# Five gate and up groups of three FFN layers as seven block products (Strassen form), with the pre-norm gain on the rows and h kept in DRAM

## Chip, cores and metric

One Trainium2 chip; the program runs on 1 of its cores. The metric is the device time of one execution in microseconds (us), the median of several runs. TensorE is written PE here, with PEld for its weight loads; VectorE is DVE, ScalarE is ACT, GpSimd is POOL and SyncE is SP, whose queue issues nearly all DMAs.

## What is computed

Two decoder layers over 512 tokens of width 1024. Each layer is: half-step SwiGLU FFN, token mixing, cross-attention, half-step SwiGLU FFN. So there are four FFNs. The part that the change touches:

```python
def half_ffn(h, l, j):
    y = swiglu(rms_norm(h, ffn_norm_pre[l, j]), ffn_w_gate[l, j], ffn_w_up[l, j], ffn_w_down[l, j])
    return h + 0.5 * rms_norm(y, ffn_norm_post[l, j])
def swiglu(x, w_gate, w_up, w_down):
    return (silu(x @ w_gate) * (x @ w_up)) @ w_down
# x: 512 x 1024;  w_gate, w_up: 1024 x 2816;  w_down: 2816 x 1024;  float32
```

## The kernel before

**Precision.** Every large product is made in three matmuls (`three`, lines 2109 to 2113): each operand is split into a rounded high part and a low part that holds the rest, and hi*lo, lo*hi and hi*hi are added in PSUM. So every weight piece has to be split on the chip before PE can use it: ACT copies the piece `raw` to `whi`, which rounds it (`split`, lines 780 to 796), and DVE makes `wlo` = raw - whi (`split`, lines 1306 to 1326). The input x is held as `xhi` and `xlo`, 8 tiles of 128 features by 512 tokens.

**Pieces.** All weights are cut into numbered pieces of 128 partitions x 1024 floats. SP loads a piece into one of four `raw` slots as two DMAs of 256 KB (`load`, line 534, issued at line 541), once the low part of the piece four before it is made. ACT, DVE and PE go through the pieces in the same order. ACT and DVE work three pieces ahead of PE (LOOKAHEAD); `whi` and `wlo` have four slots, so ACT can begin piece n when PE has finished piece n-4 (`pieces_used`). PE waits for the low part of each piece (`weights`, line 2406). Each engine runs its instructions strictly in the order written, so an instruction that waits holds back all that stand behind it on its engine.

**An FFN.** The 2816 hidden columns are 11 groups of 256. A group of gate and up is 4 pieces; a piece holds 2 of the 8 feature tiles, for 256 gate and 256 up columns. PE makes 2 x 4 column blocks x 3 = 24 matmuls of 128x512 per piece (`body` line 2478, `feature_major` line 2410), 96 per group, into four PSUM banks; two sets of banks alternate. Behind the group ACT takes silu of the gate half (line 1070), DVE multiplies it with the up half (line 1752), and the result `mid` is split in its turn. The groups come in three runs (FF_GROUPS): groups 0 to 2, then a pass `quads` that multiplies them with w_down in a Strassen form; groups 3 to 5 and a second `quads`; groups 6 to 10, whose `mid` is split plainly into `plain_hi` (ACT, line 1076) and `plain_lo` (DVE, line 1769), and then `down`, which multiplies these by w_down, adds what the quads left and ends the sub-layer.

**The pre-norm.** Three of the four FFNs (all but the first) are `scaled_rows`: when the sub-layer before them ends (`close_sublayer`, lines 852 and 1453), DVE updates h tile by tile (`update`, line 1501), ACT squares it, POOL takes the power (line 697), and ACT writes h * rstd into `y_rows` (`scale_rows`, line 877, its instruction is line 879). PE transposes the four tiles (`scaled_units`, line 2201, the matmuls are line 2193), tiles 2 and 3 of them within the first group of the FFN (`first_group`, line 2316), which runs on halves of the tokens, so with 128x256 matmuls. The gain vector of the pre-norm is not in the rows: it is multiplied into the weights, as a per-partition scale when ACT and DVE split a piece (lines 795 and 1324, two instructions of 512 elements each; a piece without a gain takes one of 1024, lines 791 and 1319).

Of the kernel before, what the change touches and what calls it, by code (L numbers as in the profile page):

```python
# [61 lines left out]
S1, S2, S3, S4, A12, A22, A11 = range(7)  # L62
NEG = -1e30
# [64 lines left out]
def build(nc, A, out):  # L128
# [18 lines left out]
    NB = 4 * SEQ  # L147
    h = place("h", [P, TT, D])
    y_at = top[0]
    y = place("y", [P, KT, SEQ])  # L150
    y_rows = place("y_rows", [P, TT, D], f32, y_at)
    x_at = top[0]
# [10 lines left out]
    h_scratch = place("h_scratch", [P, D], f32, ring_at + D * FLOAT)  # L163
    rsb = place("rsb", [P, SEQ])
    ident = place("ident", [P, P])
# [30 lines left out]
    post_gain = place("post_gain", [P, D], f32, at(7 * NB))  # L196
    level_f = place("level_f", [P, P], f32, at(7 * NB + 1024))
# [10 lines left out]
    w11 = place("w11", [P, 3, GC], f32, at(2 * MID + 2048))  # L208
    w21 = place("w21", [P, 3, GC], f32, at(7 * NB + 1024))
# [52 lines left out]
    paired = lambda t: t.rearrange("p (a b) n -> p a (b n)", b=2)  # L262
    blocks_of = lambda b0, b1: PS[:, b0:b1, :].rearrange("p a (b j) -> p (a b) j", j=P)


    def sem(name):
# [8 lines left out]
    hi_made, lo_made, pieces_used = map(sem, ("hi_made", "lo_made", "pieces_used"))  # L275

# [13 lines left out]
        "var_ready", "rstd_ready", "rstd_in_split", "mean_ready", "spread_ready", "spread_used"))  # L290

# [31 lines left out]
    STAGES = stages()  # L323

# [21 lines left out]
    def group_pieces(kind, g, n, arg=None):  # L346

        return 1 if kind == "odd_in" and ODD_COLS[g][0] == "c_f" else \
            n + 2 if arg == "late_kv" and g == 0 else n

    total_pieces = sum(group_pieces(kind, g, n, arg) for kind, _, arg, ng, n in STAGES for g in range(ng))

# [24 lines left out]
    def scaled_rows(kind, l, arg):  # L377

        return kind == "gate_up" and (l, arg[0]) != (0, 0)

# [15 lines left out]
    for kind, _, arg, ng, n in STAGES:  # L396
        if kind != "quads":
            for _ in range(sum(group_pieces(kind, g, n, arg) for g in range(ng))):
                raw_of.append(len(raw_split))
                raw_split.append(len(raw_of) - 1)  # L400
# [3 lines left out]
        raw_split += [place_of("B22", min(q + 1, QUADS - 1)) for q in range(0, QUADS, 2)]  # L404
        raw_of += [None] * n

# [49 lines left out]
    for kind, l, arg, ng, n in STAGES:  # L456
        for g in range(ng):
            for i in range(group_pieces(kind, g, n, arg)):
                gated = kind == "gate_up" or from_h(kind, arg)
# [55 lines left out]
    def _(sp):  # L515
# [18 lines left out]
        def load(n, halves):  # L534
# [3 lines left out]
            if n >= RAW_SLOTS:  # L538
                sp.wait_ge(lo_made, raw_split[n - RAW_SLOTS] + 1 + RAW_SLOTS)
# [3 lines left out]
        def load_corners(k, l, j, corners=range(3)):  # L543
# [5 lines left out]
            else:  # L549
                sp.wait_ge(lo_made, passes[k - 1][0] + len(quad_pieces()) + RAW_SLOTS)  # L550
# [52 lines left out]

        piece = ended = loads = 0
        for kind, l, arg, ng, np_ in STAGES:
            first_piece = piece
            if kind == "gate_up":
                j, n = arg
                g0 = FF_GROUPS[n][0]
                for g in range(ng):  # L610
                    for kp in range(4):
# [6 lines left out]
                        load(loads, gate_and_up(l, j, kp, (g0 + g) * 256))  # L618
                        loads += 1
                        if piece and piece + 4 * ng in pass_of and g == (2 if n == 0 else 1) and kp < 3:  # L620
                            load_corners(pass_of[piece + 4 * ng], l, j, (kp,))
                    if g == ng - 1 and not piece:
                        load_corners(0, l, j)
                piece += 4 * ng
# [33 lines left out]
            if ends_sublayer(kind, arg):  # L658
                sp.wait_ge(pieces_used, first_piece + 1 + SPLIT_SLOTS)
                if ended:  # L660
                    sp.wait_ge(post_gain_used, ended)
                sp.dma_start(post_gain[:], post_gain_rows(kind, l, arg).broadcast_to([P, D])).then_inc(post_gain_loaded, 16)
                ended += 1
        assert piece == total_pieces
# [10 lines left out]
    def _(pool):  # L675
# [58 lines left out]
        for n_stage, (kind, l, arg, ng, np_) in enumerate(STAGES):  # L734
            base_piece = E.piece
            E.piece += sum(group_pieces(kind, g_, np_, arg) for g_ in range(ng))
# [39 lines left out]
    def _(act):  # L776
# [3 lines left out]
        def split(n):  # L780
# [6 lines left out]
            act.wait_ge(raw_full[from_slot], 32 * (raw_of[n] // RAW_SLOTS + 1))  # L787
            act.wait_ge(pieces_used, n + 1)
            gains = piece_gain[n]
# [62 lines left out]
        def close_sublayer(kind, n, n_stage):  # L852
# [197 lines left out]

        mids = sums = 0
        for n_stage, (kind, l, arg, ng, np_) in enumerate(STAGES):
# [5 lines left out]
            if kind == "gate_up":  # L1058
                for g in range(ng):
                    for kp in range(4):  # L1060
                        if early and g == 0 and kp == 0:
                            E.piece += 1
                        else:
                            split_next()
                    mids += 1
                    if scaled_rows(kind, l, arg):
# [7 lines left out]
                    if arg[1] == len(FF_GROUPS) - 1:  # L1074
                        act.wait_ge(product_ready, mids)
                        a(plain_hi[:, 2 * g:2 * g + 2, :], paired(mid[:, 4:8, :]), ACT.Copy).then_inc(mid_hi_ready, 2)
# [1734 lines left out]
```

## Time and profile before

| what | value |
|---|---|
| median of 3 runs | 2311.55 us (2310.42 to 2313.16) |
| the profiled execution, from its first to its last instruction (its span) | 2311.2 us |
| PE busy | 2289.0 us, 99% |
| PEld busy | 1940.0 us, 84% |
| DVE busy | 1336.2 us, 58% |
| ACT busy | 977.3 us, 42% |
| POOL busy | 73.6 us, 3% |
| DMA: bytes, share of 16 engines' time on SP's queue | 217.70 MB, 29.0% |

No time other than its span is listed for the profiled execution. Busy time of an engine is the time in which at least one of its instructions runs. The "mean ns" of a matmul counts from its start to its modelled end and overlaps the next one, so the rate of PE is read from the starts in the timeline, not from that mean.

### The profile page before, as it was taken

The numbers are of one execution on the slowest core, as the hardware profiler recorded it, in microseconds if no ns is written. First come the engines' busy times: TensorE is split into PE (matmuls) and PEld (weight loads), VectorE is DVE, ScalarE is ACT, GpSimd is POOL, SyncE is SP. The second block draws the span as 40 slices with busy tenths as digits, with TensorE's granted clock in tenths as the row PEclk, the third lists the DMA queues.
The fourth block names the chain that finished last, engine by engine and source line by source line (L and its number), as shares of the span: only waits on it lengthen the run. The fifth ranks groups of instructions, "written<-read, shape, count | busy, mean of one in ns | idle before, by whom it ended". The sixth has DMA issues, their size and how long they took to land. (4 is left out here: it accounts for less than half of the span.)

```text
span 2311.2 us, 30089 instructions
## 1 busy us (share of the span) xinstructions
PE 2289.0 (99%) x11883; PEld 1940.0 (84%) x11883; DVE 1336.2 (58%) x1862; ACT 977.3 (42%) x1612; POOL 73.6 (3%) x115
## 2 busy tenths in 40 slices
PE   8999999999999999999999999999999999999998
PEld 7888888888888888888888888888878888888887
DVE  5857536596645646573355564346897574557334
ACT  5433324444444444443343433235266554444332
POOL 0000003000000000000010000000000000000000
PEclk9999999999999999999999999999999999999999
DMA  4332332311223223413323313333322222341321
GB/s 168 108 130 79 95 110 74 109 64 55 74 74 105 70 78 105 146 59 105 98 85 119 124 59 102 106 95 92 101 74 83 92 65 92 110 135 48 117 93 73
DMA packets 171650, 217.70 MB, mean 94 GB/s; under 512 B 13080, under 2 KB 123000, under 8 KB 171512
## 3 DMA queue, kind: packets, MB, share of 16 engines
q1 hardware_dynamic: 171400, 215.75, 29.0%
q8 instruction: 96, 1.57, 0.3%
q14 instruction: 42, 0.34, 0.0%
q10 hardware_dynamic: 112, 0.03, 0.0%
HBM read 213.63 MB, written 2.10 MB: 93 GB/s over the span
## 5 line engine op out<-in xcount | busy, mean ns | idle before, releaser
L2111 PE MATMUL ps<-xlo,whi 128*128 128x512 f32 (+1 forms) x2056 | 755.5, 367 | 2.1 <-DVE wlo L1324 2.1
L2112 PE MATMUL ps<-xhi,wlo 128*128 128x512 f32 (+1 forms) x2056 | 753.2, 366 | 0.0
L2113 PE MATMUL ps<-xhi,whi 128*128 128x512 f32 (+1 forms) x2056 | 753.0, 366 | 0.0
L1324 DVE SCALAR_TENSOR_TENSOR wlo<-raw,vec,whi 128x512 fp32r<-128x512 f32 (+1 forms) x488 | 340.8, 742 | 388.9 <-ACT whi L795 387.8
L795 ACT ACTIVATE whi<-raw,vec 128x512 fp32r<-128x512 f32 (+1 forms) x488 | 320.8, 709 | 445.4 <-PE ps L2113 390.5
L2111 PEld LDWEIGHTS ps<-xlo,whi 128*128 128x128 f32 x2056 | 388.6, 189 | 65.6 <-issue 2.7
L2113 PEld LDWEIGHTS ps<-xhi,whi 128*128 128x128 f32 x2056 | 388.4, 189 | 62.9
L2112 PEld LDWEIGHTS ps<-xhi,wlo 128*128 128x128 f32 x2056 | 388.6, 189 | 62.0
L1319 DVE TENSOR_TENSOR wlo<-raw,whi 128x1024 fp32r<-128x1024 f32 x104 | 126.7, 1223 | 183.1 <-ACT whi L791 182.3
L791 ACT ACTIVATE whi<-raw 128x1024 fp32r<-128x1024 f32 x104 | 109.5, 1057 | 199.7 <-PE ps L2113 199.3
L2111 PE MATMUL ps<-wlo,xhi 128*128 128x512 f32 x352 | 138.6, 394 | 1.0 <-issue 1.0
L2113 PE MATMUL ps<-whi,xhi 128*128 128x512 f32 x352 | 137.2, 390 | 0.0
L2112 PE MATMUL ps<-whi,xlo 128*128 128x512 f32 x352 | 137.1, 389 | 0.0
L2229 PE MATMUL ps<-wlo,mid_hi 128*128 128x512 f32 x336 | 131.6, 392 | 0.4 <-DVE wlo L1313 0.4
L2234 PE MATMUL ps<-whi,mid_hi 128*128 128x512 f32 x336 | 130.8, 389 | 0.0
L2233 PE MATMUL ps<-whi,mid_lo 128*128 128x512 f32 x336 | 130.8, 389 | 0.0
L2111 PE MATMUL ps<-wlo,plain_hi 128*128 128x512 f32 x320 | 125.0, 391 | 0.0
L2113 PE MATMUL ps<-whi,plain_hi 128*128 128x512 f32 x320 | 124.6, 389 | 0.0
L2112 PE MATMUL ps<-whi,plain_lo 128*128 128x512 f32 x320 | 124.5, 389 | 0.0
L814 ACT ACTIVATE whi<-w 128x512 fp32r<-128x512 f32 x144 | 83.3, 622 | 91.9 <-PE ps L2113 33.9
L1313 DVE TENSOR_TENSOR wlo<-w,whi 128x512 fp32r<-128x512 f32 x144 | 92.8, 685 | 35.3 <-ACT whi L814 34.4
L1752 DVE TENSOR_TENSOR mid<-mid,ps 128x1024 f32<-128x1024 f32 x33 | 40.3, 1221 | 111.9 <-ACT mid L1070 111.9
(291 smaller groups left out, 2909.5 us busy)
## 6 DMA issues: line engine op xcount, KB each, us to landing
raw<-ffn_w_gate_dram SPq DMA_DIRECT2D x176, 256.0 KB, 2.8
raw<-ffn_w_up_dram SPq DMA_DIRECT2D x176, 256.0 KB, 3.1
raw<-ffn_w_down_dram SPq DMA_DIRECT2D x96, 256.0 KB, 3.1
w<-ffn_w_down_dram SPq DMA_DIRECT2D x72, 256.0 KB, 5.3
raw<-xattn_w_kv_dram SPq DMA_DIRECT2D x64, 256.0 KB, 2.9
raw<-even_w_in_dram SPq DMA_DIRECT2D x56, 256.0 KB, 2.9
raw<-odd_w_in_dram SPq DMA_DIRECT2D x42, 256.0 KB, 2.9
raw<-xattn_w_q_dram SPq DMA_DIRECT2D x32, 256.0 KB, 3.0
```

Of the source, the lines that this page charges most:

```text
L791: a(flat(whi[:, slot]), flat(raw[:, from_slot]), ACT.Copy).then_inc(hi_made, 1)
L795: last = a(hi[:, k, :], full[:, k, :], ACT.Copy, scale=vec[:, c:c + 1])
L814: last = a(whi[:, slot, i, :], unit_source(k, name, q), ACT.Copy)
L1313: last = v.tensor_tensor(wlo[:, slot, i, :], unit_source(k, name, q), whi[:, slot, i, :].bitcast(f32), SUB)
L1319: v.tensor_tensor(flat(wlo[:, slot]), flat(raw[:, from_slot]), flat(whi[:, slot]).bitcast(f32), SUB).then_inc(lo_made, 1)
L1324: last = v.scalar_tensor_tensor(out=lo[:, k, :], in0=full[:, k, :], scalar=vec[:, c:c + 1], in1=hi[:, k, :].bitcast(f32), op0=MUL, op1=SUB)
L2111: mm(out_ap, lh, rl, start=start, stop=False, skip_group_check=skip_group_check)
L2112: mm(out_ap, ll, rh, start=False, stop=False, skip_group_check=skip_group_check)
L2113: return mm(out_ap, lh, rh, start=False, stop=stop, skip_group_check=skip_group_check)
L2229: opening = mm(out, hi, wlo[:, slot, i, :], start=fresh, stop=False, skip_group_check=True)
L2233: mm(out, lo, whi[:, slot, i, :], start=False, stop=False, skip_group_check=True)
L2234: last = mm(out, hi, whi[:, slot, i, :], start=False, stop=ends, skip_group_check=True)
```

## The change

For the five groups 6 to 10 of the three `scaled_rows` FFNs (15 groups) the product of x with the group's gate and up columns is made in seven block products in place of eight. The four corners are: x halves by features and by tokens, and weight corners B11 (upper 512 features, gate), B12 (upper, up), B22 (lower, up), B21 (lower, gate). A group is then seven units B11, T1, T2, B21, T3, B22, T4, each a piece of 128 x 1024 floats; T1 = B12 - B11, T2 = B22 - T1, T3 = T2 - B11 and T4 = B21 - T2 are made in place in the `raw` slots by DVE (`sum_corners`). A unit is 4 x 2 x 3 = 24 matmuls of 128x256 on a half of the tokens, from x itself or from one of four sums of corners of x (`s_hi`, `s_lo`). PE's new `weave`:

```diff
+            unit("B11", x, True, True)
+            unit("T1", z, True, True)
+            pe.wait_ge(product_kept, 3 * w + 1)
+            unit("T2", x, False, True)
+            unit("B21", y, True, True)
+            pe.wait_ge(product_kept, 3 * w + 3)
+            unit("T3", x, False, True)
+            unit("B22", z, False, True)
+            pe.wait_ge(c22_ready, w + 1)
+            unit("T4", x, False, True)
```

ACT (`keep` copies a product from PSUM to SBUF; `split_next` splits the unit three ahead):

```diff
+            split_next()
+            if held_mid is not None:
...
+                    plain_high(g, held)
...
+            keep(0, c11[:], x_out)
+            split_next()
...
+            keep(1, c22[:], z_out)
+            split_next()
+            act.wait_ge(mid_lo_ready, 2 * (mids - 1))
+            keep(2, c12, x_out)
+            split_next()
+            split_next()
+            act.wait_ge(c11_ready, w + 1)
+            a(c11[:], c11[:], ACT.Silu).then_inc(c11_silu, 1)
+            split_next()
+            split_next()
+            act.wait_ge(pieces_used, base + len(WOVEN_UNITS) + SPLIT_SLOTS)
+            a(c21, x_out, ACT.Silu).then_inc(gate_silu, 1)
```

DVE (its `split_next` also makes the sum for the unit four ahead):

```diff
+            split_next()
+            if held_mid is not None:
+                if plain:
+                    plain_low(g, held)
...
+            split_next()
...
+            split_next()
+            split_next()
+            dve.wait_ge(product_kept, 3 * w + 1)
+            unit_done("B21")
+            v.tensor_tensor(c11[:], y_out, c11[:], ADD).then_inc(c11_ready, 1)
+            split_next()
+            dve.wait_ge(product_kept, 3 * w + 2)
+            unit_done("T3")
+            v.tensor_tensor(c22[:], x_out, c22[:], ADD).then_inc(c22_ready, 1)
+            split_next()
+            dve.wait_ge(product_kept, 3 * w + 3)
+            unit_done("B22")
+            E.run(v.tensor_tensor(c12, z_out, c12, ADD))
...
+            v.tensor_tensor(u12, c11[:], c12, MUL)
+            split_next()
+            dve.wait_ge(gate_silu, mids).then_inc(bank_free[bank // 4], 1)
+            dve.wait_ge(c22_ready, w + 1)
+            v.tensor_tensor(c21, c21, c22[:], MUL).then_inc(product_ready, 1)
```

The low parts of B11, B21 and B22 are not made by DVE: ACT writes -raw into `wlo` ahead of its copy to `whi`, and POOL adds raw to it with an accumulating DMA of 512 KB inside SBUF, a kind that the kernel before does not issue. PE waits for that DMA (`raw_added`). The other four low parts stay with DVE.

```diff
+            if n in lo_by_dma:
+                a(flat(wlo[:, slot]), flat(raw[:, from_slot]), ACT.Copy, scale=-1.0)
...
+        def add_raw(n):
+
+            pool.wait_ge(hi_made, n + 1)
+            g.dma_start(wlo[:, n % SPLIT_SLOTS], raw[:, raw_of[n] % RAW_SLOTS], accum_op=ADD).then_inc(raw_added[n % SPLIT_SLOTS], 16)
```

A group loads four corners into the four raw slots. The slots of B11, B12, B22 and B21 are free again when the low parts of T3, T4, B22 and of B21 and T4 are made; SP loads in this order.

```diff
+                raw_split += [(unit["T3"],), (unit["T4"],), (unit["B22"],), (unit["B21"], unit["T4"])]
...
             if n >= RAW_SLOTS:
-                sp.wait_ge(lo_made, raw_split[n - RAW_SLOTS] + 1 + RAW_SLOTS)
+                for m in raw_split[n - RAW_SLOTS]:
+                    await_lo(sp, m)
```

In these three FFNs no gain is multiplied into the gate and up weights any more (all 11 groups); DVE multiplies it into the rows when the sub-layer before ends:

```diff
             if opens_scaled(n_stage):
                 update(0, take(0))
+                gain_rows(0)
                 row_variance(0)
                 update(1, take(1))
+                gain_rows(1)
                 split_next()
...
                 update(2, made)
+                gain_rows(2)
                 made = weigh(3)
...
                 update(3, made)
+                gain_rows(3)
...
-                E.run(a(y_rows[:, t, :], h[:, t, :], ACT.Copy, scale=rstd_in[:, t:t + 1]), rows_scaled)
+                E.await_(rows_gained)
+                E.run(a(y_rows[:, t, :], y_rows[:, t, :], ACT.Copy, scale=rstd_in[:, t:t + 1]), rows_scaled)
```

The four sums of x are made in the first run of groups (`token_sums` on DVE: four additions that put corners of x together, four sums, four low parts, at pieces 4 to 10; `sums_high` on ACT: four high parts). To make room, SP stores h (2 MB) to DRAM within that run and reads it back in `down`:

```diff
+        def keep_h():
...
+            sp.wait_ge(rows_scaled, TT * kept[0])
+            for half in range(2):
+                sp.dma_start(h_kept[half * HALF:(half + 1) * HALF].rearrange("(t p) d -> p t d", p=P),
+                             h[:, 2 * half:2 * half + 2, :]).then_inc(h_stored, 16)
...
+                        if scaled_rows(kind, l, arg) and n == 0 and (g, kp) == (1, 1):
+                            keep_h()
...
+                if kind == "down" and scaled_rows("gate_up", l, arg):
+                    restore_h()
```

## Rows read from the trace of the kernel before

**Rows 1.** The page: span, and busy time of each engine with its share.

```profile
span 2311.2 us, 30089 instructions
PE 2289.0 (99%) x11883; PEld 1940.0 (84%) x11883; DVE 1336.2 (58%) x1862; ACT 977.3 (42%) x1612; POOL 73.6 (3%) x115
```

**Rows 2.** Windows: busy of PE, PEld, DVE, ACT, POOL; clock, DMA share, GB/s.

```profile
858.90:923.10 64.20, 64.20 (x329) 54.92 (x328) 38.03 (x53) 26.54 (x37) 0.00 (x0) 1.00 0.31 99
1396.00:1504.80 108.80, 108.80 (x482) 90.09 (x481) 38.16 (x47) 33.54 (x44) 0.00 (x0) 1.00 0.33 102
```

**Rows 3.** Timeline of PE (start us, us), first and last of 77 consecutive matmuls.

```profile
299.67 0.39 PE L2113 MATMUL ps<-xhi,whi 128*128 128x512 f32 x1
...
316.89 0.39 PE L2111 MATMUL ps<-xlo,whi 128*128 128x512 f32 x1
```

**Rows 4.** Timeline of PE in a first group, first and last of 48 consecutive matmuls.

```profile
845.27 0.28 PE L2111 MATMUL ps<-xlo,whi 128*128 128x256 f32 x1
...
850.90 0.28 PE L2113 MATMUL ps<-xhi,whi 128*128 128x256 f32 x1
```

**Rows 5.** Timeline of ACT, two successive groups, and the instruction behind the second.

```profile
1440.31 1.06 ACT L1076 ACTIVATE plain_hi<-mid 128x1024 fp32r<-128x1024 f32 x1 [1.45 <-DVE mid L1752]
...
1462.08 1.06 ACT L1076 ACTIVATE plain_hi<-mid 128x1024 fp32r<-128x1024 f32 x1 [1.45 <-DVE mid L1752]
1463.04 1.32 ACT L795 ACTIVATE whi<-raw,vec 128x512 fp32r<-128x512 f32 x2
```

**Rows 6.** Timeline, same groups: a piece's end on PE, then ACT; DVE, then SP.

```profile
1464.61 0.39 PE L2113 MATMUL ps<-xhi,whi 128*128 128x512 f32 x1
...
1465.10 1.34 ACT L795 ACTIVATE whi<-raw,vec 128x512 fp32r<-128x512 f32 x2 [0.74 <-PE ps L2113]
...
1455.59 1.41 DVE L1324 SCALAR_TENSOR_TENSOR wlo<-raw,vec,whi 128x512 fp32r<-128x512 f32 x2 [4.02 <-ACT whi L795]
...
1457.03 0.37 SPq L541 DMA_DIRECT2D raw<-ffn_w_gate_dram  x1
1457.44 0.47 SPq L541 DMA_DIRECT2D raw<-ffn_w_up_dram  x1
```

**Rows 7.** Groups of ACT by form (count, then busy us, mean ns, idle before).

```profile
L791 ACT ACTIVATE whi<-raw 128x1024 fp32r<-128x1024 f32 x104 | 109.5, 1057 | 199.7 <-PE ps L2113 199.3 <-DVE c_v L1857 0.3
L980 ACT ACTIVATE x_v<-ps 128x512 f32<-128x512 f32 x8 | 4.8, 597 | 21.1 <-PE ps L2113 21.1
```

**Rows 8.** Groups of DVE by form.

```profile
L1319 DVE TENSOR_TENSOR wlo<-raw,whi 128x1024 fp32r<-128x1024 f32 x104 | 126.7, 1223 | 183.1 <-ACT whi L791 182.3
L1412 DVE TENSOR_TENSOR w<-w,w 128x1024 f32<-128x1024 f32 x8 | 9.8, 1226 | 0.3
L1460 DVE TENSOR_TENSOR y_rows<-ps,y_rows 128x512 f32<-128x512 f32 x32 | 21.0, 686 | 33.4 <-PE ps L2113 33.3
```

**Rows 9.** DMA issues of the whole span (count, KB each, median us to landing).

```profile
raw<-ffn_w_gate_dram SPq DMA_DIRECT2D x176, 256.0 KB, 2.8
raw<-ffn_w_up_dram SPq DMA_DIRECT2D x176, 256.0 KB, 3.1
...
h<-x_dram SPq DMA_DIRECT2D x2, 1024.0 KB, 6.2
...
post_gain<-ffn_norm_post_dram SPq DMA_DIRECT2D x4, 512.0 KB, 4.7
...
out_dram<-h SPq DMA_DIRECT2D x3, 512.0 KB, 2.6
```

**Rows 10.** The DMA view of 864 to 875 us: queue's share, one kind of issue.

```profile
q1 hardware_dynamic: 2415, 3.08, 86.3%
...
raw<-ffn_w_up_dram SPq DMA_DIRECT2D x3, 256.0 KB, 4.9
```

**Rows 11.** Timeline where an FFN opens: ACT's last row tile, PE's transposes of it.

```profile
851.68 1.14 ACT L879 ACTIVATE y_rows<-h,rstd_in 128x1024 f32<-128x1024 f32 x1
...
854.77 1.04 PE L2193 MATMUL ps<-ident,y_rows 128*128 128x128 f32 x8
```

More of the change, by code:

```diff
@@ L62 @@
 S1, S2, S3, S4, A12, A22, A11 = range(7)
+WOVEN = (6, 7, 8, 9, 10)
+WOVEN_UNITS = ("B11", "T1", "T2", "B21", "T3", "B22", "T4")
+WOVEN_SUMS = ("T1", "T2", "T3", "T4")
+WOVEN_CORNERS = ("B11", "B12", "B22", "B21")
+WOVEN_BY_DMA = ("B11", "B21", "B22")
 NEG = -1e30
@@ L609, in _ @@
                 g0 = FF_GROUPS[n][0]
+                after = piece + stage_pieces(kind, l, arg, ng, np_)
                 for g in range(ng):
@@ L735, in _ @@
             base_piece = E.piece
-            E.piece += sum(group_pieces(kind, g_, np_, arg) for g_ in range(ng))
+            for n in range(base_piece, base_piece + stage_pieces(kind, l, arg, ng, np_)):
+                if n in lo_by_dma:
+                    add_raw(n)
+            E.piece += stage_pieces(kind, l, arg, ng, np_)
             if from_h(kind, arg) and not scaled_rows(kind, l, arg):
@@ L1326, in split, with sum_corners @@
             last.then_inc(lo_made, 1)
+        def sum_corners(n):
+            if n not in sum_at:
+                return
+            count, name, unit, corner = sum_at[n]
+            b11, b12, b22, b21 = [raw[:, corner[c] % RAW_SLOTS] for c in WOVEN_CORNERS]
+            if name == "T1":
+                await_raw(dve, corner["B11"])
+                await_raw(dve, corner["B12"])
+                ins = v.tensor_tensor(flat(b12), flat(b12), flat(b11), SUB)
+            if name == "T2":
+                await_raw(dve, corner["B22"])
+                await_lo(dve, unit["T1"])
+                ins = v.tensor_tensor(flat(b12), flat(b22), flat(b12), SUB)
+            if name == "T3":
+                await_lo(dve, unit["B11"])
+                dve.wait_ge(corners_summed, count - 1)
+                ins = v.tensor_tensor(flat(b11), flat(b12), flat(b11), SUB)
+            if name == "T4":
+                await_raw(dve, corner["B21"])
+                await_lo(dve, unit["T2"])
+                dve.wait_ge(corners_summed, count - 1)
+                ins = v.tensor_tensor(flat(b12), flat(b21), flat(b12), SUB)
+            ins.then_inc(corners_summed, 1)
         def split_next():
@@ L1708, in _, with plain_low, block_sums @@
         lambda_sums()
+        def plain_low(g, mids):
+            dve.wait_ge(mid_hi_ready, 2 * mids)
+            v.tensor_tensor(plain_lo[:, 2 * g:2 * g + 2, :], paired(mid[:, 4:8, :]),
+                            plain_hi[:, 2 * g:2 * g + 2, :].bitcast(f32), SUB).then_inc(mid_lo_ready, 2)
+        def block_sums(mids):
+            dve.wait_ge(product_ready, mids)
+            a12, a22, a11, a21 = [mid[:, 4 + n, :] for n in range(4)]
+            E.run(v.tensor_tensor(mid[:, S1, :], a21, a22, ADD))
+            first_sum = E.last
+            E.run(v.tensor_tensor(mid[:, S3, :], a11, a21, SUB))
+            dve.wait_ge(*first_sum)
+            E.run(v.tensor_tensor(mid[:, S2, :], mid[:, S1, :], a11, SUB))
+            E.own()
+            v.tensor_tensor(mid[:, S4, :], a12, mid[:, S2, :], SUB).then_inc(sums_ready, 1)
@@ L2437, in forget_gates, with weave, unit @@
             return last
+        def weave(w, bank):
+            base, x, y, z = woven_base[w], bank, bank + 1, bank + 2
+            if E.made["s_used"] == 0 or w == woven_first_of(w):
+                E.made["s_used"] += 1
+                pe.wait_ge(s_lo_ready, 4 * E.made["s_used"])
+            corner_of = {"B11": (0, 0), "B21": (4, 0), "T4": (4, 1)}
+            sum_of = {"T1": 0, "T2": 1, "T3": 2, "B22": 3}
+            def unit(name, bank, start, stop):
+                n = base + WOVEN_UNITS.index(name)
+                weights(n)
+                wh, wl = [t[:, n % SPLIT_SLOTS].rearrange("p a (b n) -> p (a b) n", n=256) for t in (whi, wlo)]
+                if name in corner_of:
+                    hi, lo = [token_half(t, *corner_of[name]) for t in (xhi, xlo)]
+                else:
+                    hi, lo = s_hi[:, sum_of[name]], s_low(sum_of[name])
+                for k in range(4):
+                    for c in range(2):
+                        cols = slice(c * P, (c + 1) * P)
+                        last = three(PS[:, bank, c * HALF:(c + 1) * HALF], wh[:, k, cols], wl[:, k, cols],
+                                     hi[:, k, :], lo[:, k, :], start and k == 0 and c == 0,
+                                     stop and k == 3 and c == 1, skip_group_check=True)
+                last.then_inc(pieces_used, 1)
+            unit("B11", x, True, True)
[8 more added lines that the diff above has]
+            unit("T4", x, False, True)
         T = nc.tensor.transpose
```

315 lines of the change are left out of this document (251 added, 64 removed).

## Prediction

> **What bounds the kernel now.** I read the page first: PE has work for 2289.0 of the 2311.2 us, DVE and ACT for about half of it [rows 1]. So PE's stream is the time, and no other engine's work counts until PE waits for it. Then the windows by stage: in groups 6 to 10 of an FFN PE runs through all of 108.80 us, five groups of 21.76 us at a granted clock of 1.00 (2.4 GHz), with DVE at 38.2 and ACT at 33.5 us [rows 2] (the other window there is an FFN's first run of groups); the period shows too in ACT's `plain_hi`, 1440.31 and 1462.08 [rows 5]. Last the starts of single matmuls, for the busy means overlap. 128x512: (316.89 - 299.67)/76 = 0.2266 us each [rows 3], so a group is 96 x 0.2266 = 21.76 us. 128x256, the form that the change uses: (850.90 - 845.27)/47 = 0.1198 us [rows 4], not 0.1133: each matmul has a fixed part.
>
> **What PE can gain.** A group becomes 7 x 24 = 168 matmuls of 128x256. At 0.120 us a unit is 2.88 us and a group 20.16 us, 1.60 less than 21.76. Fifteen groups: 24.0 us, 8.0 per FFN. That is the whole gain: an eighth of the columns goes, and over a third of it is given back in fixed parts of the narrower matmuls.
>
> The Trainium skill (TensorE: Matmul & The Clock Gate, Part 1, "Wait — 56ns, not 53.3ns?") puts the warm spacing at columns over 2.4 GHz and some 2.5 ns. By it the groups would be 96 x 215.8 and 168 x 109.2 ns, 2.37 us apart, and the gain 35.6 us. The starts in this trace give 226.7 and 119.8 ns, some 13 ns of fixed part at either width; the measurement decides.
>
> **What has to arrive in time.** PE now eats a unit per 2.88 us where a piece lasted 5.44, so splits, loads and sums come at nearly twice the rate, and three new waits stand in PE's stream. Durations: ACT 1.06 us for 1024 elements, 0.60 for 512 from PSUM [rows 7]; DVE 1.22 for a low part, 1.23 for a sum in place, 0.69 for 512 from PSUM [rows 8]. Back to back about 0.1 less (1463.04 - 1462.08 = 0.96 [rows 5]). Hand-offs: PE's last matmul of a 128x512 piece starts at 1464.61 and ACT at 1465.10, 0.26 after the next matmul is due at 1464.84; DVE to SP 0.03 (1455.59 + 1.41, 1457.03) [rows 6]; about 0.1 between ACT and DVE and 0.15 to PE, my estimate from these.
> Load per group: ACT 3 x 2.1 (two copies for B11, B21, B22) + 4 x 1.06 + 3 x 0.6 (`keep`) + 2 x 0.6 (silu) + 1.06 = 14.6 us; DVE four sums 4.9, four low parts 4.9, five operations of 512 3.4, `plain_lo` 1.2 = 14.4 us. Both fit into 20.16; the order decides. I wrote the orders of ACT, DVE, SP and POOL against PE's, PE starting a group at 0. Two chains hardly close.
>
> Chain A, the raw slot. T2 ends at 8.64; +0.26; ACT `keep` 0.50 and T4's high part 1.06: 10.46. DVE +0.13 + 1.22: 11.81. Now SP may reload the slot with the next group's B12: 0.41 us between the pair's issues + 3.1 to landing = 3.5 [rows 6, 9]: 15.34. DVE, which has stood waiting, +0.1 + 1.22 for the next T1: 16.65. Only behind it in DVE's order is the addition into c22, 0.60: 17.25, +0.15 to PE: 17.40. PE wants it for T4 at 6 x 2.88 = 17.28. So A lacks 0.1 us when a pair lands in 3.5, and each us later costs PE a us, at four of an FFN's five groups (the last loads no corner).
>
> Chain B, the accumulating DMA, D us from ACT's high part to its arrival. From A's 16.65: T1's high part 17.8, low part 19.2, T2's sum 20.5, its high part at 1.5 of the next group, silu 2.0, B21's two copies 3.8, POOL 3.9. PE wants B21 at 8.64, so D must be under 4.7. By the same count B22's copies end at 8.6 for 14.40, D under 5.7, and the next B11's at 13.8 for 20.16, D under 6.2. A wait in front of B21 also gives chain A that much, so a group loses the larger of (pair - 3.4) and (D - 4.7), not both; over 5.7 the other two limits add.
>
> **Unknown prices.** The pair: 3.5 alone; beside the w_down corners, with the queue's share at 86%, the second half took 4.9, a pair 5.3 [rows 10]. In my order the data of B12's pair run between B22's accumulation and B11's and touch the tail of one: I take 4.0, ends 3.5 and 5.3. D: no row has such a DMA. Below stands a store of 512 KB from SBUF, 2.6; above, twice the bytes read, the 1 MB load, 6.2, with 0.5 for the issue and 0.6 of waiting for the other transfers, 7.3 [rows 6, 9]. The nearest row in size is the 512 KB load, 4.7; with 0.5 for an issue I take D = 5.2, ends 2.6 and 7.3. Nothing below these counts: PE cannot start sooner than its stream lets it.
> At 4.0 and 5.2 a group loses 0.6 (A and B alike), an FFN 5 x 0.6 = 3.0 of the 8.0. Net 5.0 per FFN, 15.0 in all.
>
> **The rest.** (1) Opening of the three FFNs: DVE gets four multiplications of 1024, some 1.2 us each, between update and variance. ACT's square of the tile runs beside the first; by my count tile 3 reaches ACT 1.6 us later, at 853.3 for 851.68, is done at 854.4, and PE takes it at 854.77 [rows 11]: covered by 0.3. Tile 1 is up to 0.6 late. 0.5 per FFN; ends 0 and 1.6. (2) The sums of x: twelve operations of 1.2 us, 14.7, on DVE, less 0.19 for each of 12 pieces without a gain (1.41 against 1.22 [rows 6, 8]), so 12.4 onto 38.0 in a window of 64.2 [rows 2]. Cover: DVE's three-piece lead. If it is used up, the first pieces of `quads` are late. 0.3 per FFN; ends 0 and 2. (3) h, 2 MB out and back on SP's queue, at 1 MB per 6.2 [rows 9], 13 us each way: piece 6's load stands behind it with some 13 us to spare, `post_gain` with a whole first half of `down`. Nothing; if the cover fails it shows in (2). (4) DVE's and ACT's shorter splits, where PE does not wait: nothing.
> Sum: 15.0 - 3 x 0.8 = 12.6 us. 2311.2 - 12.6 = 2298.6; the median stands 0.35 above the profiled span, so 2299.0.
>
> **Rivals.** (a) No wait to speak of: D under 4.7 and a pair in 3.5. Only 0.1 per group is lost, and 24.0 - 1.5 - 1.5 = 21 us gained: 2290. For it: a 512 KB store takes 2.6. Against: two chains must close to a tenth of a us.
> (b) The pair comes late: at 5.3 a group loses 1.9, four groups 7.6, and the FFN gains 0.4; with (1) and (2) the time is 2312, no change. For it: 4.9 was seen whenever transfers bunched, and a group now moves 1.5 MB more inside SBUF. The Trainium skill (DMA: Bandwidth & Descriptors, "Issuing engines are not separate DMA queues") says that transfers of all issuers run on the same 16 engines and interleave; the row of 86% shows it for one queue, none for two. Against: the accumulations are short, and most lie beside no load.
> (c) Slower: the accumulating DMA is the bound, PE waiting before B21, B22 and B11 each time. It decides from D = 6.7, where the 8.0 per FFN are used up (by the three limits about 1.7 per group, and 1 at the first B11). At D = 7 an FFN loses 2.4, at D = 8 10.3: with 2.4 for (1) and (2), 2321 and 2345. For it: two reads and a write per float, descriptors written by POOL, and ACT's two copies ahead. Against: 512 KB rows of 2.6 and 4.7.
> That PE does less work than the starts in rows 4 say, or more, I leave out: the form is the same.
>
> **Chances.** Forecast 0.35, (a) 0.20, (b) 0.15, (c) 0.30. A measurement here tells 0.2%, 4.6 us, from no change. Faster 0.55, same 0.15, slower 0.30. The range goes from (a)'s best, all 24 us, 2288, to 2330, between D = 7 and 8; what D over 7.5 leaves out has about 0.15. Faster and slower both hold weight: the likeliest case's own range is 2292 to 2306.
>
> **What would show it.** Right: 168 matmuls of 0.120 us per group; groups 6 to 10 of a scaled FFN in some 104 us for 108.8; PE's waits on DMA `wlo` and on DVE `c22`, some 0.6 per group; POOL's DMA landing in 5 us; B12's pair in 4. Chain A wrong: no PE wait on c22 although pairs land after 4. Chain B wrong: B11 or B22 are waited for and not B21. The rest wrong: PE waits over 1 us per FFN on y_rows, or on `wlo` or `mid_lo` where `quads` begins. Wrong altogether: D over 6.7.

## The result, and the profile after

The changed kernel takes **2317.09 us** (median; 2313.86 to 2320.65) where the kernel before takes 2311.46 beside it: a ratio of 1.0025, 95% interval 1.0015 to 1.0034, so 5.6 us slower where 12.6 us less were forecast. The time lies in the range; the direction is wrong.

The page of the changed kernel: span, busy times, and the two DMA queues that move data (packets, MB, share of 16 engines' time).

```profile
span 2314.6 us, 32573 instructions
...
PE 2270.2 (98%) x12963; PEld 1972.9 (85%) x12963; DVE 1464.9 (63%) x1898; ACT 1061.6 (46%) x1642; POOL 115.0 (5%) x160
...
q1 hardware_dynamic: 175096, 229.90, 30.6%
q0 software_dynamic: 6480, 23.60, 5.3%
```

Against [rows 1], PE has 18.8 us less work but a longer span: it now waits. DVE has 129 us more, ACT 84, POOL 41. The second queue is new: 45 accumulating DMAs, 23.6 MB.

Windows of the changed kernel over groups 6 to 10 of the three FFNs (columns as in rows 2).

```profile
1034.93:1145.43 110.50, 101.95 (x842) 101.05 (x841) 68.67 (x70) 66.32 (x78) 12.04 (x14) 1.00 0.67 167
1397.26:1508.15 110.89, 104.28 (x842) 102.71 (x842) 69.72 (x71) 66.17 (x78) 11.91 (x14) 0.98 0.68 167
2146.61:2252.74 106.13, 102.24 (x841) 101.17 (x840) 69.11 (x71) 66.03 (x78) 11.91 (x14) 1.00 0.70 172
```

In the kernel before each of these stretches takes 108.80 us [rows 2]. Now they take 327.5 in all for 326.4, so the 24.0 us that the columns should have given are gone within the stretch itself. The DMA share there has doubled, 0.33 to about 0.68.

PE's waits by what ended them (us in total, times, longest).

```profile
PE ps L2447 <- DMA wlo<-raw: 15.7, 12, 3.1
...
PE ps L2447 <- DVE c L2023: 2.6, 2, 1.3
PE ps L2529 <- ACT y_rows L988: 2.2, 3, 1.8
PE ps L2447 <- DVE wlo L1503: 2.1, 3, 1.5
```

One row carries it: the accumulating DMA, 15.7 us in the whole span. By the order of PE's matmuls nine of its 12 waits, 14.4 us, stand before B11, two before B21 (1.1 us) and one before B22 (0.2). The second pair of rows, y_rows and `wlo` of DVE, stands where the FFNs open. Where successive stages begin on PE tells the same: over the three stretches from the first run of groups' `quads` to `down` the two kernels differ by 1.1 us, over the three openings (from the sub-layer before to the first `quads`) by 0.8, 2.7 and 0.8, together 4.3. 1.1 + 4.3 is the 5.6 that was measured, within 0.2. (The two spans differ by 3.4 only, since the start-up, ahead of all that was changed, was 2.1 us shorter in this profiled execution.)

The timeline where the last group of the first scaled FFN begins (start us, us, engine): SP, POOL, DVE, then PE.

```profile
1113.17 2.36 SPq L608 DMA_DIRECT2D raw<-ffn_w_up_dram  x4
1115.63 0.93 SPq L608 DMA_DIRECT2D raw<-ffn_w_gate_dram  x2
...
1115.88 0.85 POOL L792 DMA_DIRECT2D wlo<-raw  x1 [4.82 <-ACT whi L899]
...
1116.66 1.22 DVE L1522 TENSOR_TENSOR raw<-raw 128x1024 f32<-128x1024 f32 x1 [2.38 <-DMA raw<-ffn_w_up_dram]
...
1121.83 0.28 PE L2449 MATMUL ps<-xhi,whi 128*128 128x256 f32 x1
1125.21 0.36 PE L2447 MATMUL ps<-xlo,whi 128*128 128x256 f32 x1 [3.09 <-DMA wlo<-raw]
```

And the DMA view of 1115.88 to 1125.08 us in the same trace, from the issue of B11's accumulation to its landing (loads on q1, accumulations on q0).

```profile
q1 hardware_dynamic: 1172, 1.12, 41.1%
q0 software_dynamic: 144, 0.52, 28.9%
...
raw<-ffn_w_gate_dram SPq DMA_DIRECT2D x2, 256.0 KB, 6.2
wlo<-raw POOLq DMA_DIRECT2D x1, 512.0 KB, 9.2
```

At 1113.17 the raw slot of B12 comes free, and within 3.4 us SP issues three pairs of corners at once: B12's pair, and those of B22 and B21, whose slots had been free or came free just then. POOL issues B11's accumulation at 1115.88, in the middle of them. In the 9.2 us to its landing the loads take 41.1% of the 16 engines, 3.8 us, and the accumulation 28.9%, 2.7 us. The accumulation issued at 1059.65, with hardly a load beside it, has the same 2.7 us of work and lands after 4.4; this one lands 4.8 later. PE, done with its unit at 1121.95, waits until 1125.21.

The landings of all 45, in the order B11, B21, B22 of each group (us from issue):

```
FFN 2:  4.6 4.4 4.4 | 7.7 4.4 4.4 | 8.5 4.4 4.7 | 7.5 6.2 4.4 | 9.2 4.4 4.4
FFN 3:  5.1 4.4 6.0 | 5.9 5.0 5.4 | 6.8 4.4 4.4 | 8.7 4.4 5.4 | 6.2 5.1 5.4
FFN 4:  4.4 4.4 5.2 | 6.4 4.4 4.4 | 8.0 4.4 4.4 | 7.4 4.4 5.1 | 6.6 4.4 4.8
```

Alone such a DMA lands in 4.4. All those of B21 and B22 land in 4.4 to 6.2, and so does B11's in the first group of a run, ahead of which no corners are due. B11's in the twelve other groups take 5.9 to 9.2. POOL's issue is not what differs: it takes 0.84 to 1.05 us in all 45.

### The profile page after: what moved, and what is told of

Same layout as the page of the kernel before. It is cut to its first block and busy times, and to the rows that moved or that the text cites. A ratio compares the mean times of both kernels' runs of the same rounds, so it can differ in the third digit from the quotient of the medians.

```text
span 2314.6 us, 32573 instructions
## 1 busy us (share of the span) xinstructions
PE 2270.2 (98%) x12963; PEld 1972.9 (85%) x12963; DVE 1464.9 (63%) x1898; ACT 1061.6 (46%) x1642; POOL 115.0 (5%) x160
## 5 line engine op out<-in xcount | busy, mean ns | idle before, releaser
L2447 PE MATMUL ps<-xlo,whi 128*128 128x512 f32 (+1 forms) x1936 | 672.0, 347 | 22.2 <-DMA wlo<-raw 15.5
L2448 PE MATMUL ps<-xhi,wlo 128*128 128x512 f32 (+1 forms) x1936 | 668.3, 345 | 0.0
L2449 PE MATMUL ps<-xhi,whi 128*128 128x512 f32 (+1 forms) x1936 | 668.0, 345 | 0.0
L1503 DVE TENSOR_TENSOR wlo<-raw,whi 128x1024 fp32r<-128x1024 f32 x236 | 287.8, 1223 | 319.2 <-ACT whi L899 317.3
L899 ACT ACTIVATE whi<-raw 128x1024 fp32r<-128x1024 f32 x281 | 295.3, 1054 | 398.3 <-PE ps L2449 295.7
L2447 PEld LDWEIGHTS ps<-xlo,whi 128*128 128x128 f32 x1936 | 367.2, 190 | 70.5 <-issue 20.8
L1509 DVE SCALAR_TENSOR_TENSOR wlo<-raw,vec,whi 128x512 fp32r<-128x512 f32 (+1 forms) x224 | 154.9, 737 | 154.2 <-ACT whi L903 153.5
L903 ACT ACTIVATE whi<-raw,vec 128x512 fp32r<-128x512 f32 (+1 forms) x224 | 145.4, 702 | 198.0 <-PE ps L2449 163.2
L2448 PE MATMUL ps<-s_hi,wlo 128*128 128x256 f32 x480 | 135.8, 283 | 0.0
L2449 PE MATMUL ps<-s_hi,whi 128*128 128x256 f32 x480 | 135.8, 283 | 0.0
```

The costliest lines, as they stand in the source:

```text
L899: a(flat(whi[:, slot]), flat(raw[:, from_slot]), ACT.Copy).then_inc(hi_made, 1)
L903: last = a(hi[:, k, :], full[:, k, :], ACT.Copy, scale=vec[:, c:c + 1])
L1503: v.tensor_tensor(flat(wlo[:, slot]), flat(raw[:, from_slot]), flat(whi[:, slot]).bitcast(f32), SUB).then_inc(lo_made, 1)
L1509: last = v.scalar_tensor_tensor(out=lo[:, k, :], in0=full[:, k, :], scalar=vec[:, c:c + 1], in1=hi[:, k, :].bitcast(f32), op0=MUL, op1=SUB)
L2447: mm(out_ap, lh, rl, start=start, stop=False, skip_group_check=skip_group_check)
L2448: mm(out_ap, ll, rh, start=False, stop=False, skip_group_check=skip_group_check)
```

## The experiments

**Theory 1:** B11's accumulation meets the six corner loads of its own group and lands too late; this eats the gain. **Theory 2:** the openings cost 4 us, for the multiplications by the gain stand in front of the variance. Rivals: the accumulations as such do not pay; chain A, the raw slot, is the bound; DVE has too much to do altogether.

### B11's low part by DVE

```diff
-WOVEN_BY_DMA = ("B11", "B21", "B22")
+WOVEN_BY_DMA = ("B21", "B22")
```

> Edit: B11's low part is made by DVE again; B21 and B22 keep the accumulating DMA. Theory 1 (collision: B11's accumulation lands late only because SP issues the next group's B12, B22 and B21 loads, 1.5 MB, just before it): PE's waits on DMA wlo at the first unit of a group go (they were 0.5 to 3.1 us there), the 30 accumulations left land in 4.4 to 5.5 us, the five groups of an FFN take 102 to 104 us, and the time is 16 to 19 us under the changed kernel's: 2298 to 2302, faster than before. Rival A (an accumulating DMA is too slow wherever it stands): the waits move to B21 and B22 and the time stays at 2310 to 2317. Rival B (the slot chain through c22 binds once B11 is out of the way): waits on c22 of 1 us or more per group, gain under 6 us: 2311 to 2316.

Measured: 2303.29 us, ratio 0.9959 (0.9944 to 0.9974). PE's waits of this kernel:

```profile
PE ps L2529 <- ACT y_rows L988: 2.2, 3, 1.8
PE ps L2447 <- DMA wlo<-raw: 2.1, 5, 1.1
PE ps L2447 <- DVE wlo L1503: 2.1, 3, 1.5
...
PE ps L2447 <- DVE c L2023: 1.6, 2, 1.3
```

14 us come back, and the change is faster than the kernel before by 0.4%; the time is 1.3 us over the range expected. The wait for the accumulation falls from 15.7 to 2.1 us; that for c22, chain A, does not grow, though DVE has 1.2 us more per group. The openings' rows stand as they were. (The profiled execution of this kernel took 2299.59, 3.7 under its median.)

### The corner loads held back

SP loads B22's and B21's corners only when B11's accumulation has landed.

```diff
+                            wg = woven_group[n_stage, g]
+                            if kp == 2 and wg % len(WOVEN):
+                                await_lo(sp, woven_base[wg])
```

> Edit: SP holds the next group's B22 and B21 loads back until B11's accumulation has landed (not at an FFN's first woven group). Theory 1 (collision): the 12 accumulations of B11 behind a woven group land in 4.4 to 6.5 us, not in 5.9 to 9.2, and PE's wait in front of B11 goes; the corner B22 comes some 5 us later, so PE waits for T2 or T3 instead, about 3 us per group, and the time is 2325 to 2340. Rival A (B11's accumulation is slow for another reason than the loads): its landing stays at 6 to 9 us.

One execution: 2343.21 us. The twelve accumulations of B11 that had taken 5.9 to 9.2 now land in 4.4 to 5.3, one in 6.3: the loads, not the accumulations of the same group, had held them up. The price is larger than what it cures, for the corners are now late:

```profile
PE ps L2450 <- ACT c L1198: 27.2, 12, 4.0
...
PE ps L2450 <- DMA wlo<-raw: 2.9, 6, 0.9
```

It is some 3 us above the expectation. The trace shows one part that the expectation did not have: seven times, after a wait, PE runs 15 to 22 matmuls at the lower clock (below, in the last section), 10.8 us in all.

### No block products, the rest of the change

```diff
-WOVEN = (6, 7, 8, 9, 10)
+WOVEN = ()
```

> Edit: no group is woven (eight block products as before); the gain on the rows, the sums of x and h's way through DRAM stay. Theory 2 (what the change costs outside groups 6 to 10 is the gain multiplication ahead of the variance where an FFN opens, about 4.3 us in three openings by the stage starts of the two traces): 2315 to 2317, PE's added waits on y_rows and on wlo within the openings, none where quads begin. Rival C (the sums of x and the 2 MB of h cost as much): waits at the first quads of an FFN too, 2318 or more. Rival D (the openings cost little, and the loss is all in the woven groups): 2311 to 2313.

Measured: 2315.81 us, ratio 1.0017 (1.0008 to 1.0027), with only the waits of the openings left:

```profile
PE ps L2529 <- ACT y_rows L988: 2.2, 3, 1.8
PE ps L2447 <- DVE wlo L1503: 2.1, 3, 1.5
...
PE ps L2529 <- DVE h L1719: 0.8, 1, 0.8
```

So gain on the rows, sums of x and h in DRAM cost 4.2 us together, and the groups themselves about 1.4 in the changed kernel. PE waits nowhere for a sum of x or for the DMAs of h; and from tile 3's transposes to the first `quads` of an FFN it takes 58.8 us in this kernel as in the kernel before, so these are hidden.

### No accumulating DMA

```diff
-WOVEN_BY_DMA = ("B11", "B21", "B22")
+WOVEN_BY_DMA = ()
```

> All seven low parts of a group are made by DVE, none by an accumulating DMA; the rest is the changed kernel (2317). Theory: DVE then has seven low parts (8.6 us), four sums (4.9), five operations of 512 (3.4) and plain_lo (1.2), 18.1 us for a group of 20.16, in an order that waits; the addition into c22 comes late and PE waits on it some 1.5 to 2 us per group, so nearly all of the 24 us are lost again and, with the openings at 4.2, the time is 2312 to 2320: the DMAs for B21 and B22 do pay, only B11's does not. Rival: the DMAs never paid, DVE has room, and the time is at or under the 2303 of the kernel with B11 alone on DVE.

Measured: 2311.41 us, ratio 0.9997 (0.9987 to 1.0006).

```profile
PE ps L2447 <- DVE c L2023: 12.1, 12, 1.7
```

With seven low parts on DVE the addition into c22 comes late in all twelve groups that have a next one, 1.0 us each (1.5 to 2 was expected, so the time is just under the range). The accumulations of B21 and B22 thus pay some 8 us (0.9997 to 0.9959), and that of B11 costs 14.

### The addition into c22 first

On DVE, beside B11's low part: the addition into c22 ahead of the next group's T1 sum.

```diff
-            split_next()
+            split(E.piece + LOOKAHEAD)
...
             v.tensor_tensor(c22[:], x_out, c22[:], ADD).then_inc(c22_ready, 1)
+            sum_corners(E.piece + LOOKAHEAD + 1)
+            E.piece += 1
```

> B11's low part by DVE, and on DVE the addition into c22 stands ahead of the next group's T1 sum, which waits for a pair of corners. By the prediction's chain A a late pair delays c22 and PE's T4: then PE's waits on DVE c (1.6 us) go away and the time falls by up to 1.5 us, to 2301.8. Rival: T1's sum is then late for its own unit and the wait only moves: 2303 to 2304, with waits on wlo of DVE in place of c.

Measured: 2302.22 us, ratio 0.9959 (0.9947 to 0.9972): no difference from 0.9959.

```profile
PE ps L2449 <- DMA wlo<-raw: 3.4, 7, 0.9
```

The waits on `c` are gone (1.6 before), those on `wlo<-raw` have grown from 2.1 to 3.4. The rival was right that the wait moves, but it moves to the accumulations of B21 and B22 and not to a low part of DVE; probably, which is not shown, because T1's sum is later, and with it the units behind it on ACT and POOL's issue.

### The gain left out, and the gain behind the power

The first leaves out the multiplication of the rows by the pre-norm gain in three FFNs; the second multiplies it together with rstd, and ACT's scaling goes away. Both have B11's low part on DVE. The second's edit:

```diff
-                E.run(a(y_rows[:, t, :], y_rows[:, t, :], ACT.Copy, scale=rstd_in[:, t:t + 1]), rows_scaled)
...
             def gain_rows(t):
...
-                E.run(v.tensor_tensor(y_rows[:, t, :], h[:, t, :], pre_gain[:], MUL), rows_gained)
+                E.await_(input_rstd_ready)
+                E.run(v.scalar_tensor_tensor(out=y_rows[:, t, :], in0=h[:, t, :], scalar=rstd_in[:, t:t + 1],
+                                             in1=pre_gain[:], op0=MUL, op1=MUL), rows_scaled)
...
                 update(0, take(0))
-                gain_rows(0)
                 row_variance(0)
-                update(1, take(1))
-                gain_rows(1)
+                add_second(1)
+                gain_rows(0)
+                update(1, weigh(1))
                 split_next()
                 row_variance(1)
+                gain_rows(1)
```

> B11's low part by DVE (2303.3 before this run), and the four multiplications of the rows by the pre-norm gain are left out, so that three FFNs are computed without that gain; ACT scales h straight into y_rows as in the kernel before. If the four operations on DVE are the price of the openings (4.2 us in all), the time falls by 3 to 4 us, to 2299 to 2300.5, and PE's waits on y_rows go from 2.2 us to 0.3. If the openings are long for another reason (POOL's power taking longer beside DVE's one-operation split of a piece without a gain, the sums of x, the traffic of h), it falls by under 1 us.

> B11's low part by DVE, and the gain is multiplied in the same DVE operation as rstd, behind POOL's power, in place of ACT's scaling (one scalar_tensor_tensor per tile; ACT's four operations of 1.15 go away). Path of a tile: update, square, variance, power, one operation of about 1.28: that of the kernel before but for 0.13. If the gain in front of the variance is the price, 2299 to 2301, with PE's wait on tile 1's y_rows gone (1.8 to under 0.5). If DVE's load is the price, wherever it stands, 2302.5 to 2304, as without it.

Measured: 2297.40 us, 0.9938 (0.9925 to 0.9950), without the gain; 2297.72 us, 0.9937 (0.9925 to 0.9950), with the gain behind the power. In both, each of the three openings is as long as in the kernel before, within 0.6 us: from PE's first transposes to the first `quads` 78.3, 79.7 and 78.3 us without the gain, 78.3, 80.4 and 78.3 with it behind the power, 78.4, 80.3 and 78.4 before, and 79.2, 82.9 and 79.2 in the changed kernel. So the price of the openings was not the 14.7 us of the operations on DVE, for the second kernel has as many there, but where they stand in a tile's chain. (That kernel also saves ACT's scaling and one hand-off; the place by itself was not tested.) The two times are 5.9 and 5.6 us under that with B11 alone on DVE, and 1.6 and 1.3 under the ranges expected; by the ratios the fall is 4.9 and 5.1, which the intervals do not tell from the 4.3 of the openings. In the second opening, in the changed kernel (DVE, ACT, PE):

```profile
1192.95 1.28 DVE L1719 SCALAR_TENSOR_TENSOR h<-y_rows,rstd,h 128x1024 f32<-128x1024 f32 x1 [0.52 <-POOL rstd L787]
1194.27 1.22 DVE L1727 TENSOR_TENSOR y_rows<-h,pre_gain 128x1024 f32<-128x1024 f32 x1
1195.41 1.22 DVE L1503 TENSOR_TENSOR wlo<-raw,whi 128x1024 fp32r<-128x1024 f32 x1
1196.55 0.15 DVE L1760 TENSOR_SCALAR var_in<-h_squares 128x1 f32<-128x1 f32 x1
...
1197.35 1.15 ACT L988 ACTIVATE y_rows<-y_rows,rstd_in 128x1024 f32<-128x1024 f32 x1 [0.96 <-POOL rstd_in L797]
...
1198.64 0.30 PE L2529 MATMUL ps<-ident,y_rows 128*128 128x128 f32 x1 [1.81 <-ACT y_rows L988]
```

and with the gain behind the power:

```profile
1186.99 1.28 DVE L1711 SCALAR_TENSOR_TENSOR h<-y_rows,rstd,h 128x1024 f32<-128x1024 f32 x1 [0.50 <-POOL rstd L787]
1188.19 1.22 DVE L1495 TENSOR_TENSOR wlo<-raw,whi 128x1024 fp32r<-128x1024 f32 x1
1189.49 0.15 DVE L1753 TENSOR_SCALAR var_in<-h_squares 128x1 f32<-128x1 f32 x1
1190.30 1.28 DVE L1719 SCALAR_TENSOR_TENSOR y_rows<-h,rstd_in,pre_gain 128x1024 f32<-128x1024 f32 x1 [0.66 <-POOL rstd_in L797]
...
1191.73 0.30 PE L2521 MATMUL ps<-ident,y_rows 128*128 128x128 f32 x1 [0.28 <-DVE y_rows L1719]
```

and in the kernel before:

```profile
1192.38 1.28 DVE L1506 SCALAR_TENSOR_TENSOR h<-y_rows,rstd,h 128x1024 f32<-128x1024 f32 x1 [0.50 <-POOL rstd L692]
...
1197.00 1.06 PE L2193 MATMUL ps<-ident,y_rows 128*128 128x128 f32 x8 [0.65 <-ACT y_rows L879]
```

In the changed kernel tile 1 needs 5.69 us from the start of its update to PE's transposes, with gain and split both between update and variance; PE waits 1.81 for it. With the gain in the operation behind the power it needs 4.74, and PE waits 0.28. In the kernel before it is 4.62, and PE waits 0.65.

### The variance first, and what POOL waits for

In the changed kernel, the variance of tiles 1 and 3 ahead of DVE's split; then, in a second kernel, also the two `xlo` operations, which read PSUM, between tile 1's variance and the split. The edit for tile 1, in the first kernel and in the second:

```diff
                 gain_rows(1)
+                row_variance(1)
                 split_next()
-                row_variance(1)
                 open_lo(0, x_banks[0])
```

```diff
                 gain_rows(1)
-                split_next()
                 row_variance(1)
                 open_lo(0, x_banks[0])
+                split_next()
```

> Edit: in the opening DVE makes the row variance of tiles 1 and 3 ahead of the split of the next piece, not behind it; all else as in the changed kernel. Theory 2: the variance of tile 1 comes about 1.1 us sooner, and PE's waits on y_rows (2.2 us and 0.8 us on h, in three openings) fall to under 1.5 together: 2314.5 to 2316.5, a gain of 0.5 to 2.5. If the row chain is not what PE waits for there, no change (2316 to 2318); if the late split is wanted first, waits on wlo grow and it is slower.

> The changed kernel with the variance of tile 1 ahead of DVE's split, and behind it the two xlo operations, which read PSUM, before the split. Theory: POOL's one-column power takes 0.54 us where DVE runs no two-input operation from SBUF to SBUF without a scalar beside it, and waits for the end of such a one otherwise (1.46 beside the split in the run with the variance first alone). So tile 1's power in the middle opening goes from 1.46 to 0.54 and PE's wait there from 1.6 to about 0.7; the time, in one look, 2315 to 2318. Rival: the power's length has another cause (a longer gap before it, or its turn of two) and stays 0.9 or more.

The first: 2318.64 us, ratio 1.0026 (1.0015 to 1.0037), nothing gained. Its timeline, DVE and POOL:

```profile
1199.17 0.15 DVE L1760 TENSOR_SCALAR var_in<-h_squares 128x1 f32<-128x1 f32 x1
1199.24 1.22 DVE L1503 TENSOR_TENSOR wlo<-raw,whi 128x1024 fp32r<-128x1024 f32 x1
...
1199.41 1.46 POOL L797 TENSOR_TENSOR rstd_in<-var_in,neg_half 128x1 f32<-128x1 f32 x1 [2.85 <-DVE var_in L1760]
```

The variance comes 1.2 us sooner, but POOL's power of one column now lies beside DVE's split and takes 1.46 us for 0.54; it ends 0.4 after the split. In the second kernel (one execution, 2316.05 us):

```profile
1194.49 0.15 DVE L1760 TENSOR_SCALAR var_in<-h_squares 128x1 f32<-128x1 f32 x1
1194.98 1.29 DVE L1563 TENSOR_TENSOR xlo<-ps,xhi 128x512 fp32r<-128x512 f32 x2 [0.33 <-ACT xhi L934]
1196.18 1.22 DVE L1503 TENSOR_TENSOR wlo<-raw,whi 128x1024 fp32r<-128x1024 f32 x1
...
1194.72 0.55 POOL L797 TENSOR_TENSOR rstd_in<-var_in,neg_half 128x1 f32<-128x1 f32 x1 [2.85 <-DVE var_in L1760]
```

0.55 us again, and PE's wait for tile 1 in this opening falls from 1.64 in the first to 0.75, near the 0.65 of the kernel before and as expected. The time hardly moves: the opening's other two waits, 0.77 on DVE's update of h and 1.58 on a low part of DVE, are as in the first.

### Both orders

B11's low part by DVE, the gain behind the power and the addition into c22 first.

> Both together: B11's low part by DVE, the gain multiplied with rstd in one DVE operation, and the addition into c22 ahead of the next group's T1 sum. Against 2297.7 without the last: if the waits on c22 are PE's own (2.1 us there), 2296 to 2297; if they only move to B21's and T1's low parts, as the run with c22 first alone showed, 2297 to 2298.5.

Measured: 2297.01 us, ratio 0.9937 (0.9924 to 0.9951): the same as without the new order on DVE. PE's waits on c22 (2.1 us) are gone, those for the accumulations have grown from 1.3 to 2.8: again they only move. The version with the gain behind the power, or this one, beats both kernels: 15 us under the kernel before and some 20 under the changed one.

## Why the prediction was wrong, point by point

**The rate of PE** held. 168 matmuls per group were counted at 0.120 us; in the kernel with B11 on DVE the 840 matmuls of a stretch start 0.1207 us apart on the mean outside the waits (0.1198 in rows 4), so the 24.0 us became 326.4 - 2520 x 0.1207 = 22.2.

**D, the accumulating DMA alone**, was taken as 5.2 with ends 2.6 and 7.3; alone it is 4.4, under chain B's limit of 4.7 for B21. So B21, where the sum had 0.6 us per group, is waited for twice, 1.1 us in all. Its issue on POOL is 0.85 us and not the 0.5 taken.

**The step that failed** is the overlap of the accumulations with the loads: the sum has one D, 5.2, for all 45, from a 512 KB load and an issue, with nothing in it for other transfers (the 0.6 for those stands in the upper end alone); and in rival (b) "the accumulations are short, and most lie beside no load". The prediction's own count had the next group's B12 pair "between B22's accumulation and B11's", touching one tail. It took SP's loads one pair at a time. But all of B12, B22 and B21 wait in one queue behind B12's slot: when that comes free, six loads go out in 3.4 us, and B11's accumulation is issued into them. Its D is 5.9 to 9.2 against chain B's limit of 6.2. The limit was right. PE's nine waits before B11 are 1.6, 2.4, 1.4, 3.1 | 0.7, 2.8 | 0.2, 1.9, 0.3 us in the order of the table; D - 6.2 there is 1.5, 2.3, 1.3, 3.0 | 0.6, 2.5 | 0.2, 1.8, 0.4. Of the three that are not waited for two land in 5.9 and 6.2, and the third, 7.4, follows a wait of 1.3 on c22 that covers it. Rival (c) named the bound, with the wrong accumulations: it wanted all three late at D = 6.7, and one late, at 7.4 on the mean, sufficed. "B11 or B22 are waited for and not B21" was given as the sign that chain B is wrong. That came but for two waits, though the chain's limits held: B21's accumulations were just quicker than the sum had them and B11's slower.

The Trainium skill (DMA: Bandwidth & Descriptors, "Issuing engines are not separate DMA queues") says that transfers from all issuers share the 16 engines and interleave. The prediction had it for rival (b) alone, with no row for two queues. The DMA view above is that row, and it agrees: 3.8 us of loads and 2.7 of the accumulation in the same 9.2 us, for a landing of 4.4 alone. The rule should have been applied to each accumulation with the loads issued at that moment.

**Chain A** exists but was put too high, at 0.6 us per group: where B11's DMA is not the bound and DVE's order is the changed kernel's, PE waits on c22 two to four times, 1.6 to 2.7 us in all twelve groups. In the kernel without accumulations, where DVE makes seven low parts per group, it is the bound, with 1.0 us per group.

**(1) The openings** were put at 0.5 us per FFN with ends 0 and 1.6; they cost 0.8, 2.7 and 0.8, the second beyond the upper end. "ACT's square of the tile runs beside the first" holds for tile 0, but at tiles 1 and 3 DVE's split stands ahead of the variance too. In the kernel before the split alone lay beside the square; now gain and split, 2.3 us, stand beside a square of 1.2. And POOL's power lengthens where DVE's split lies beside it. The prediction said of tile 3 "covered by 0.3" from one FFN's rows and of tile 1 "0.6 late"; in the second opening PE waits 1.81 on tile 1, 0.77 on DVE's update of h and 1.47 on a low part of DVE, where the kernel before has 0.65, 0.38 and 0.40. For tile 3 it waits in none.

**(2), (3), (4)**, the sums of x, h in DRAM and the shorter splits: no wait in PE's stream can be put down to them; the kernel without the products, 4.2 us above, has only the waits of the openings. That the first `quads` of an FFN begins 0.8, 2.6 and 0.8 later in it, counted from the first transposes, belongs to the opening: all of it has come about by tile 3's transposes, and it is gone with the gain behind the power.

**The sum** as it came: 22.2 us less of PE's work; 23.3 us of waits in the three stretches, from PE's starts (18 gaps, 21.8 us over the usual spacing, and 1.5 at the lower clock, below); 4.3 us in the openings. 22.2 - 23.3 - 4.3 = 5.4 us slower.

## What to carry to other kernels

A DMA on which the bound engine waits is to be costed with all transfers that are issued in the microseconds around it, by any engine: write down what each queue releases at the moment when a buffer comes free, for a queue that stood behind one wait sends all that stood there at once (here six loads in 3.4 us). Where an operation is moved into a chain of engines, try it in the operation that ends the chain and not in front of the hand-offs, and see what the neighbouring engine runs beside it.

## What was not expected of the hardware

**POOL beside DVE.** The pre-norm's power of one column took 0.54 us in all 12 places before. Where a DVE operation of 1024 elements with two inputs from SBUF began before it and is still running, it takes 1.45 to 1.53 us and ends 0.4 after that operation; beside one that reads PSUM it keeps 0.54. The kernel before shows this already, in the post-norm's power beside a DVE operation of 512:

```profile
1184.82 0.69 DVE L1471 TENSOR_TENSOR y_rows<-y_rows,post_gain 128x512 f32<-128x512 f32 x1
...
1184.98 0.92 POOL L692 TENSOR_TENSOR rstd<-var,neg_half 128x1 f32<-128x1 f32 x1 [333.61 <-DVE var L1464]
```

In the twelve traces 229 powers of one column began while such an operation ran, and took 0.92 to 1.53 us; the 299 others took 0.53 to 0.56. The expectation for the kernel with the two `xlo` operations ahead of the split had it that a scalar operand makes the difference; the kernel with the gain behind the power refutes that: there POOL's power lies beside DVE's update of h, which has one. DVE and POOL of that kernel:

```profile
1200.58 0.15 DVE L1753 TENSOR_SCALAR var_in<-h_squares 128x1 f32<-128x1 f32 x1 [0.55 <-ACT h_scratch L938]
1200.66 1.28 DVE L1711 SCALAR_TENSOR_TENSOR h<-y_rows,rstd,h 128x1024 f32<-128x1024 f32 x1
...
1200.82 1.53 POOL L797 TENSOR_TENSOR rstd_in<-var_in,neg_half 128x1 f32<-128x1 f32 x1 [0.38 <-DVE var_in L1753]
```

The Trainium skill (Trainium Architecture — The Big Picture, "What this means for kernel authors") states that the port pair which these two engines share in SBUF is an exclusive lock, and that nothing else contends on the engines' side. The rows agree with the lock, with 0.54 and 1.53 us; that nothing else contends no row here shows. Nor is this what delays B11's accumulation: in the first 1.4 us after the issue of B21's accumulations DVE runs up to 1.1 us of such operations, after B11's at most 0.6, and yet it is B11's that land late.

**PE's clock after a wait.** Windows of the changed kernel around one wait for the accumulation (2.81 us, ended at 1464.18):

```profile
1461.00:1465.00 4.00, 1.19 (x10) 1.01 (x9) 3.97 (x6) 2.12 (x3) 0.00 (x0) 0.96 0.35 91
1465.00:1469.00 4.00, 4.00 (x24) 4.00 (x24) 2.16 (x2) 2.50 (x4) 0.85 (x1) 0.61 0.24 48
1469.00:1473.00 4.00, 4.00 (x36) 4.00 (x35) 2.36 (x2) 2.73 (x4) 0.00 (x0) 1.00 0.47 91
```

After it 16 matmuls start 0.213 us apart in place of 0.120, at the lower of the two levels, 1.2 GHz, until the clock rises again at 1468.15; that is 1.5 us on top of the wait. It does not follow each long wait: the one of 3.09 us that ended at 1125.21 is followed by matmuls at 0.12. In these stretches of the kernel with the loads held back it happens seven times, of that with B11 on DVE not once in the profiled execution. That it is behind the wide spread of the changed kernel's times, 2313.9 to 2320.7, is not shown, for only one execution of each is traced; the mean granted clock of its seven executions points that way, 0.997 in the fastest and 0.994 to 0.996 in the others.
